# A hybrid encoder step on one core: the sample's values in plain fp32 on two column halves, and instructions moved in their engines' order

## The reference, cut to what matters

```python
h = rms_norm(x, g_mix)
z = h @ w_in
q_f, k_f, v_f, f_logit, c_q, c_kv, k_r = jnp.split(z, offs, axis=-1)
logf = jax.nn.log_sigmoid((f_logit + b_f).astype(jnp.float32))
q_m = (rms_norm(c_q, g_cq) @ w_uq).reshape(B, T, MLA_HEADS, MLA_NOPE_DIM + MLA_ROPE_DIM)
ckv = rms_norm(c_kv, g_ckv)
cum = jnp.cumsum(logf, axis=1)
fox_o = attend_blocks(fox_q, fox_k, fox_v, pos, pos, FOX_SCALE, 1, cum, cum)
mk, mv = mla_keys_values(ckv, kr, w_ukv)
mla_o = attend_blocks(mla_q, mk, mv, pos, pos, MLA_SCALE, CHUNK)
mixed = jnp.concatenate([rms_norm(fox_o, g_fox_out), rms_norm(mla_o, g_mla_out)], axis=-1)
x = x + mixed @ w_o            # then a cross-attention into memory, and a SwiGLU
```

## Time and profile before

| | |
|---|---|
| median of 3 runs | 819.49 us (819.45 to 819.50) |
| profiled execution | 820.14 us |
| its span, first to last instruction | 818.1 us |
| TensorE busy | 799.3 us, 98% of the span |
| VectorE, ScalarE, POOL busy | 66%, 50%, 40% |
| share of the last-ending chain on TensorE | 89% |

### The profile page before, as it was taken

How to read it: one execution, slowest core, us unless ns; L and a number is a source line. 1 busy time by engine, 2 the same in 40 slices (tenths; PEclk the granted TensorE clock), 3 DMA queues, 4 the chain that set the end, 5 groups by cost and what they waited for, 6 DMA issues and landing times.

```text
span 818.1 us, 15951 instructions
## 1 busy us (share of the span) xinstructions
PE 799.3 (98%) x5842; PEld 761.5 (93%) x5842; DVE 543.1 (66%) x986; ACT 408.2 (50%) x752; POOL 329.1 (40%) x242
## 2 busy tenths in 40 slices
PE   6999999899999999999999999999999999999996
PEld 6987998788887999998999999999999999999996
DVE  5344466777779747467599999988889985212213
ACT  7433565566678335464475554555554564322221
POOL 3663953373212125650564323333323346443420
PEclk9999999999999999999999999999999999999998
DMA  8333432200025333430133322332222332423103
GB/s 251 114 114 114 152 99 68 61 20 28 27 79 195 102 103 106 128 104 27 52 103 104 104 68 86 103 103 103 100 64 92 103 116 72 116 71 97 46 2 115
DMA packets 26518, 75.90 MB, mean 93 GB/s; under 512 B 2896, under 2 KB 7448, under 8 KB 26328
## 3 DMA queue, kind: packets, MB, share of 16 engines
q1 hardware_dynamic: 26176, 74.87, 28.8%
q10 hardware_dynamic: 288, 0.30, 0.1%
HBM read 68.62 MB, written 6.53 MB: 92 GB/s over the span
## 4 chain that ended last, share of the span: by engine, by line
PE 89%; DVE 4%; ACT 3%; issue 2%; DMA 1%; POOL 1%; SPq 0%; DVEq 0%; ACTq 0%
PE ps L499 27%; PE ps L500 26%; PE ps L501 26%; PE ps L658 2%; PE ps L676 2%; PE ps L926 1%; PE ps L517 1%; DMA wraw<-w_front 1%; ACT whi L1121 1%; PE ps L641 1%; POOL wlo L2241 1%; PE ps L640 1%; DVE xb L2215 1%; PE ps L911 1%; ACT probs L1121 0%
## 5 line engine op out<-in xcount | busy, mean ns | idle before, releaser
L499 PE MATMUL ps<-hhi,whi 128*128 128x288 f32 (+1 forms) x896 | 267.3, 298 | 7.0 <-DVE hlo L1609 5.8
L500 PE MATMUL ps<-hhi,wlo 128*128 128x288 f32 (+1 forms) x896 | 265.7, 297 | 0.0
L501 PE MATMUL ps<-hlo,whi 128*128 128x288 f32 x800 | 237.1, 296 | 0.0
L1121 ACT ACTIVATE whi<-wraw 128x1024 fp32r<-128x1024 f32 (+3 forms) x138 | 115.0, 839 | 133.3 <-PE ps L501 114.3
L499 PEld LDWEIGHTS ps<-hhi,whi 128*128 128x128 f32 x896 | 169.4, 189 | 8.7 <-DVE hlo L1609 5.7
L500 PEld LDWEIGHTS ps<-hhi,wlo 128*128 128x128 f32 x896 | 169.1, 189 | 0.2
L501 PEld LDWEIGHTS ps<-hlo,whi 128*128 128x128 f32 x800 | 150.9, 189 | 0.0
L2384 POOL TENSOR_TENSOR wlo<-wraw,whi 128x512 fp32r<-128x512 f32 x60 | 78.5, 1323 | 146.9 <-ACT whi L1121 146.9
L2241 POOL TENSOR_TENSOR wlo<-wraw,whi 128x256 fp32r<-128x256 f32 (+2 forms) x83 | 88.4, 1094 | 99.1 <-ACT whi L1121 99.0
L501 PE MATMUL ps<-hidlo,whi 128*128 128x288 f32 (+2 forms) x352 | 104.0, 296 | 0.0
L2398 POOL TENSOR_TENSOR wlo<-wraw,whi 128x1024 fp32r<-128x1024 f32 (+1 forms) x24 | 59.3, 2478 | 72.9 <-ACT whi L1121 72.9
(11 more groups left out here) (292 smaller groups left out, 1789.1 us busy)
## 6 DMA issues: line engine op xcount, KB each, us to landing
wraw<-w_ff SPq DMA_DIRECT2D x44, 512.0 KB, 4.0
wraw<-w_front SPq DMA_DIRECT2D x41, 512.0 KB, 3.7
wraw<-w_down SPq DMA_DIRECT2D x16, 512.0 KB, 3.6
wraw<-w_down SPq DMA_DIRECT2D x8, 384.0 KB, 3.1
wraw<-w_front SPq DMA_DIRECT2D x7, 384.0 KB, 3.4
xa<-x_t SPq DMA_DIRECT2D x8, 288.0 KB, 4.3
xs<-x_t SPq DMA_DIRECT2D x7, 288.0 KB, 6.2
out_fox_k<-kt SPq DMA_DIRECT2D x4, 288.0 KB, 2.6
```

Source lines behind the costliest of these rows:

```text
L499: nc.tensor.matmul(out, lh, rh, start=start, stop=False)
L500: nc.tensor.matmul(out, ll, rh, start=False, stop=False)
L501: return nc.tensor.matmul(out, lh, rl, start=False, stop=stop)
L1121: return nc.scalar.activation(out, src, func, **kw)
```

## The change

First, the sample tile of the values. A tile `hs` holds the 64 sample tokens of x times the gain of the first norm, in fp32, made by one VectorE instruction after the last square sum. `sample_part(b)` runs at the head of each value block and computes the sample's values for its two k tiles with plain fp32 matmuls straight from the raw block: for each k, weights `hs[:, k, :]` (64 columns), once with the raw block's left 256 columns into partitions 0 to 63 of bank 4 and once with the right 256 columns into partitions 64 to 127. It counts on the semaphore `p_part` (which takes the place of `d_half` at the kernel's end, with 5 for 1). The three fp32r matmuls of the sample tile go. The sum over partitions for the sample tile is done twice, for both halves of the partitions, and the eviction is two instructions of 256 columns. Since TensorE now reads the raw block, `load(b)` of blocks 9 to 12 waits for `p_part` as well.

Second, the order. On ScalarE the cast of block 2 comes before tile 5 of `hhi` and not after it, and the cast of block 22 is at tick 38, not 36 (its low part on VectorE at 39, not 37). On VectorE the product on `tabq` comes before three of the gate operations, the eviction of tick 23 comes before the maximum of tick 24, and the low part of tile 0 of the first attention's output is at tick 29, not 27.

```diff
+    hs, c2 = place("hs", [128, KT, TS], F32, rbase + rsize - 2 * NK * 4)
...
-            columns(0, sqacc).then_inc(n_col, 1)
+            columns(0, sqacc, 4)
+            for e in range(2):
+                mm = nc.tensor.matmul(ps[64 * e:64 * e + 64, 0, 4:5], sqacc[:, TP:T], ones[:, 0:1], start=True, stop=True)
+            mm.then_inc(n_col, 1)
...
+            def sample_part(b):
+
+                for k in (2 * (b - B_V), 2 * (b - B_V) + 1):
+                    for e in range(2):
+                        at = 512 * (k % 2) + 256 * e
+                        mm = nc.tensor.matmul(ps[64 * e:64 * e + 64, 4, 0:256], hs[:, k, :], wraw[:, b % 2, at:at + 256],
+                                              start=k == 0, stop=k == 7)
+                mm.then_inc(p_part, 1)
+
+            pe.wait_ge(s_init, 2)
...
                 pe.wait_ge(f_lo, b + 1)
+                sample_part(b)
                 for kk in range(2):
                     k = 2 * c + kk
-                    for tt in range(TT):
-                        a, n = 128 * tt, tok(tt)
-                        mm = product(ps[0:n, tt, :], [t[:, k, a:a + n] for t in x1],
+                    for tt in range(4):
+                        a = 128 * tt
+                        mm = product(ps[:, tt, :], [t[:, k, a:a + 128] for t in x1],
                                      [front(b, lo, 2, 512)[:, kk, :] for lo in (0, 1)], k == 0, k == 7)
...
             for j in range(KT):
+                if j == 5:
+                    split(2)
                 act.wait_ge(s_x[j], 16)
...
-                if j in (1, 5, 7):
+                if j in (1, 7):
                     split((j + 1) // 2 - j // 5)
...
-            SPLIT_AT = {2: 16, 4: 17, 8: 18, 13: 19, 18: 20, 23: 21, 36: 22, 46: 23, 52: 24, 59: 25, 68: 26, 73: 27, 82: 28, 86: 29,
+            SPLIT_AT = {2: 16, 4: 17, 8: 18, 13: 19, 18: 20, 23: 21, 38: 22, 46: 23, 52: 24, 59: 25, 68: 26, 73: 27, 82: 28, 86: 29,
...
             add_square(7)
+            v.tensor_tensor(hs[:, :, :], xs[:, :, TP:T], gains[:, G_MIX:G_MIX + KT].unsqueeze(2).to_broadcast([128, KT, TS]), ALU.mult)\
+                .then_inc(s_init, 1)
             dve.wait_ge(s_hlo, KT)
+            dve.wait_ge(s_init, 2)
             v.memset(vst[64:128, 6, :], 0.0).then_inc(s_init, 1)
...
             v.tensor_copy(bias[:, 0, :], ncum[:, :]).then_inc(s_ncum, 1)
+            dve.wait_ge(s_lrow, 1)
+            v.tensor_tensor(tabq[:, :], tabq[:, :], rows2(6), ALU.mult).then_inc(s_lat, 1)
...
-            dve.wait_ge(s_lrow, 1)
-            v.tensor_tensor(tabq[:, :], tabq[:, :], rows2(6), ALU.mult).then_inc(s_lat, 1)
...
+            for e in range(2):
+                a = slice(64 * e, 64 * e + 64)
+                mm = v.tensor_scalar(vst[0:64, 4, 256 * e:256 * e + 256], ps[a, 4, 0:256], small[a, S_RCM + 4:S_RCM + 5], None, ALU.mult)
+            mm.then_inc(s_vev, 1)
...
-            LOW_AT = (27, 32, 42, 52, 72, 78, 84, 90)
+            LOW_AT = (29, 32, 42, 52, 72, 78, 84, 90)
...
             for s in range(LAST + 1):
+                if s == 24:
+                    evicted(s - 1)
                 if s < TICKS:
                     maxima(s)
...
-                if s - 1 in CHUNKS:
+                if s - 1 in CHUNKS and s != 24:
                     evicted(s - 1)
...
                 need(sp, f_lo, b - 1)
+                if B_V + 2 <= b < B_V + 6:
+                    sp.wait_ge(p_part, b - B_V - 1)
```

More of the change, by code:

```diff
@@ L202, in build @@
     bias, _ = place("bias", [8, 3, NK], F32R, rbase + 2 * rsize)
+    hs, c2 = place("hs", [128, KT, TS], F32, rbase + rsize - 2 * NK * 4)
+    assert c2 <= rbase + rsize - NK * 4
     qt, _ = place("qt", [128, T], F32, sqbase)
@@ L325, in build @@
         w_vec, w_copy, t_f, x_hf, s_dsc = sem("w_vec"), sem("w_copy"), sem("t_f"), sem("x_hf"), sem("s_dsc")
-        s_y, s_yst, d_half, s_xg = sem("s_y"), sem("s_yst"), sem("d_half"), sem("s_xg")
+        s_y, s_yst, p_part, s_xg = sem("s_y"), sem("s_yst"), sem("p_part"), sem("s_xg")
         past = slice(T, NK)
@@ L1109, in _ @@
                 if half == 0:
-                    mm.then_inc(d_half, 1)
+                    mm.then_inc(p_part, 1)
             pe.wait_ge(r_sq, 16 + KT + 1)
@@ L1190, in _ @@
             act.wait_ge(s_cv, 48)
-            act.wait_ge(s_init, 2)
+            act.wait_ge(s_init, 3)
             for t in (5, 6):
@@ L1708, in _ @@
             used(dve, B_V + 3)
[L1709 to L1712, removed]
+            for tt in range(4):
+                v.tensor_scalar(vst[:, tt, :], ps[:, tt, :], small[:, S_RCM + tt:S_RCM + tt + 1], None, ALU.mult).then_inc(s_vev, 1)
+            for e in range(2):
+                a = slice(64 * e, 64 * e + 64)
+                mm = v.tensor_scalar(vst[0:64, 4, 256 * e:256 * e + 256], ps[a, 4, 0:256], small[a, S_RCM + 4:S_RCM + 5], None, ALU.mult)
+            mm.then_inc(s_vev, 1)
             def query_dup(c):
@@ L1854, in memory_key @@
                 v.tensor_tensor(kmf[:, m, 0:NM], ps[:, m, 0:NM], rmem[:, :], ALU.mult).then_inc(s_mkev, 1)
-            REST_AT = {5: 17, 9: 18, 14: 19, 19: 20, 24: 21, 37: 22, 47: 23, 53: 24, 60: 25, 69: 26, 75: 27, 83: 28, 87: 29, 88: 30, 93: 31, 94: 32}
-            LOW_AT = (27, 32, 42, 52, 72, 78, 84, 90)
+            REST_AT = {5: 17, 9: 18, 14: 19, 19: 20, 24: 21, 39: 22, 47: 23, 53: 24, 60: 25, 69: 26, 75: 27, 83: 28, 87: 29, 88: 30, 93: 31, 94: 32}
+            LOW_AT = (29, 32, 42, 52, 72, 78, 84, 90)
             QUERY_DUP_AT = {1: 2, 2: 3, 9: 4, 10: 5, 19: 6, 20: 7}
@@ L2218, in _ @@
             low, high = slice(0, LAST_AT[1]), slice(LAST_AT[1], T)
-            dve.wait_ge(d_half, 1)
+            dve.wait_ge(p_part, 5)
             residual(KT - 1, KT - 1, low, ps[:, 6, 0:low.stop], lambda a: a)
@@ L2431, in _ @@
                 load(b)
-            sp.wait_ge(s_init, 2)
+            sp.wait_ge(s_init, 3)
             sp.wait_ge(s_sq, KT)
```

## The result

The changed kernel takes 822.82 us (median of 6 runs, 822.33 to 823.58) against 819.50 us of the kernel before on the same chip: ratio 1.0041, 95% interval 1.003 to 1.0052, so 3.3 us slower. I had forecast 818.7 us within 816.8 to 820.2, and gave "slower" 0.06. The forecast was wrong, above the top of its range.

The account below looks back on a forecast made before the run. TensorE, working in 98% of the span, was taken as the bound. Terms 0 (block 2), -0.1 (value stage), 0 (block 12) and -0.7 (attention) gave -0.8 us, so 818.7 us on the median, range 816.8 to 820.2.

Parts of the forecast that it names:

- What the product frees: Value blocks on TensorE: fp32 pairs cost 0.92 us per block, saving 0.47 us each, 1.9 us over four.
- The late load, the chain and the wait of 2 us: Value stage: block 10's late load delays the gate chain; TensorE waits about 2.0 us for `tabq`; net -0.1 us.
- It holds by 0.3 us: Block 12: POOL's low part ready at 87.3, TensorE wants it about 87.6; counted 0, at most +0.8 us.
- its 0.56 us goes: Attention: with block 22's cast moved later, TensorE's 0.56 us wait at 180.72 for ScalarE's copy disappears.
- Nothing from the cast of block 2: Start: the 0.86 us wait goes, about 1 us in all, but later delays take it back; 0, bounds -1.1 and +0.5.
- The eviction of tick 23 and the low part of tile 0: Attention: normalisation 1.0 us earlier, wait at 162.95 down 0.8 us, later waits take most back; 0.15 us left.
- C: Slower: block 10's load lands late, POOL's order equally late; no gain from about 5 us, 821.1 at 6.2; chance 0.09.
- the terms at block 12 (+0.8) and in the attention (0): Block 12's low part counted 0, at most +0.8 us; attention moves summed to -0.7 us, bounds 0 and -1.6.
- wrong: Signs against the forecast: `tabq` wait under 1 us, TensorE at block 4 clearly before 27.5, block 10's load over 5 us.

Follow-up runs that it names:

- after: The changed kernel itself, against the kernel before: 822.82 us, ratio 1.0041; run and traced again in a later group: 823.35 us, ratio 1.0048.
- before: The kernel before, without the change: 819.50 us; run again for a second trace: 820.06 us, ratio 1.0006.
- pool_first: The changed kernel with one edit on POOL, the low part of block 12 ahead of `ckvlo`: 821.77 us, ratio 1.0023 to the kernel before.
- value_only: The changed kernel with the five order moves undone and the fp32 value product kept: 827.22 us, ratio 1.0094 to the kernel before.
- c22_back: The changed kernel with block 22's cast back at tick 36 and its low part at 37: 822.82 us, ratio 1.0035 to the kernel before.
- split2_back: The changed kernel with the cast of block 2 back behind tile 5: 823.26 us, ratio 1.0051 to the kernel before.
- masks_early: The changed kernel with the two mask loads ahead of the load of block 11: 823.21 us, ratio 1.0044 to the kernel before.

## Why the prediction was wrong, step by step

By the account, the value stage came out 0.55 us worse than the sum had it (0.75 with the 0.2 us ahead of it), POOL's row behind it 1.65 us, block 22 1.6 us, and small differences 0.3 us: 4.3 us between -0.8 and +3.5.

- **What the product frees.** Too large. I took a pair as 0.46 us from a row of four pairs, 512 to 128 columns wide; two pairs of 256 columns take 1.02 us from their start to the next matmul's, not 0.92. The two rows together (2.30 us for 1280 columns, 1.02 for 512) give 1.67 ns per column and some 0.17 us for each such group, an estimate; my scaling by columns left the second part out. A block saves 0.3 to 0.4 us, not 0.47: 1.3 us over four. In after it mattered little, since three blocks' saving goes into the wait anyway.
- **The late load, the chain and the wait of 2 us.** Right: 2.01 us measured. The start of the load was off by 0.3 us and its length by 0.3 us, which makes 0.56 us; 0.1 us less saved in block 10 and 0.2 us by which the second trace of before is ahead of the first make the rest of +0.7.
- **The step that failed first: "It holds by 0.3 us, if the store is not slowed by the loads of block 12 and the masks, which now go out just before it. I count 0 for it."** The store was slowed, by 1.5 us; `ckvlo` came at 84.29, not 82.5, and the low part of block 12 at 89.05, not 87.3. I had seen the collision, put it into an if-clause, and priced it at zero with 0.3 us of margin. And in the sum I followed POOL's row only one step, to block 12, although it runs without a gap to the key half that the first scores need; `ckvlo` at 82.5, 2.7 us late, would already have been 0.3 us beyond the slack of 2.4 us. Together 1.6 us. `pool_first` shows it: one line on POOL gives 1.6 us back.
- **The step that failed second: "its 0.56 us goes. VectorE's low part moves with it, out of the way of a maximum."** The first half held (0.73 us). The low part landed beside POOL's subtraction and took 2.60 us. I had used this very effect, with its row, for tile 6 at the start, and for block 21, and did not ask it of the instruction that was moved. 1.6 us off.
- **Nothing from the cast of block 2.** Right in size. The mechanism I gave is in the trace (the low part of tile 5 takes 1.84 us, at 15.30, beside POOL), and in four traces TensorE waits 0.5 to 0.8 us for block 3. A second reason I had not: the wait of 0.86 us is there only when TensorE's clock rises early. That the second reason holds on average was not measured.
- **The eviction of tick 23 and the low part of tile 0.** Right in size, -0.15 us, and by the path I gave as far as the 1.0 us gained at the normalisation and VectorE's row behind it, which took it back. The last step went otherwise: the wait near 163 fell from 1.19 to 0.88 us, not by 0.8, and it is now for ScalarE's exponentials (`probs`), not for a copy. That the sizes agree to 0.01 us is partly luck.
- **The rivals.** C was nearest, with POOL's order late in earnest. I tied it to a landing over 5 us and gave it 0.09; the landing was 4.09 us, and `ckvlo` was late by 4.7 us, 1.5 us of it by the store. The range ended at 820.2 although C stood at 821.1, and the upper bounds of the terms at block 12 (+0.8) and in the attention (0) were each too near. None of the signs that I had named as "wrong" came: the wait for `tabq`, the load under 5 us, the start and the places in the attention were all as forecast. No sign had been set on POOL's row at 88 and 103, or on VectorE's behind 184, and the loss was there.

## What to carry to other kernels

When a change makes a chain later, follow each engine on it to the next place where the bounding engine meets it, and work out the slack there, also where the profile before shows no wait. A clause "if the transfer is not slowed" is a term with a price, not a condition. And for an instruction that is moved, look at what the other engines do at its new place: here the same subtraction took 1.05 or 2.60 us by where it stood.

## What the runs showed of the hardware

- **TensorE's clock after a wait is not the same from run to run.** In the kernels with a wait near 2 us or more for `tabq` (after in both groups, `value_only`, `c22_back`, `split2_back`, `pool_first`, `masks_early`), the mean granted clock of a run was 0.995 or less in 20 of 43 runs; in those without one it was never below 0.996 in 57 runs. Of the seven traces with such a wait, the clock fell behind waits of 1.94, 2.16, 2.57 and 5.64 us and stayed up behind 1.93, 2.01 and 2.37 us. The 1.94 and the 2.01 us are the two traces of after, with the same work ahead. Where POOL does not hide it, it shows: in `pool_first` the five runs at 0.994 or 0.995 took 821.8 to 822.8 us, the five at 0.997 or 0.998 took 820.3 to 821.4 us.
- **Nor is its rise at the start.** In the 14 traces half pace ended between 9.0 and 11.7 us after the span's start, though the first matmul started between 5.5 and 6.0 us in all of them; in the two traces of after it ended at 9.5 and 11.5 us. A wait shortly behind the start hides this: the kernel before begins block 2 at 18.09 us with an early rise and a wait of 0.86 us, and at 18.02 us with a late one and none. So taking such a wait away can give less than its length shows.
- **A store that follows a load closely takes longer.** The 576 KB store of `ckvf` took 3.8 to 3.9 us with no load of 512 KB in the 12 us ahead of it, 5.1 to 5.6 us when one went out 2.5 to 2.6 us ahead, and 6.1 to 6.6 us at 1.7 us.
- **Who released a wait called "issue"** could be read here only from the other engines' rows: its end lay within 0.1 us of the end of POOL's instruction in every trace that had it.
